# Three of twelve modulation quads summed on the Vector engine from a buffer of their own, with TensorE's chunks in two others; low weights of the last key-value pairs ahead of a rotation

## The reference

```python
silu_c = jax.nn.silu(c)
silu_cctx = jax.nn.silu(c_ctx)
for i in range(DEPTH_2):
    sh1, sc1, g1, sh2, sc2, g2 = jnp.split((silu_c @ mod_w[i] + mod_b[i])[:, None, :], 6, axis=-1)
    a_lat = modulate(rms_norm(h_lat, norm_mix_g[i]), sh1, sc1)
    csh1, csc1, cg1, csh2, csc2, cg2 = jnp.split(silu_cctx @ mod_w[i] + mod_b[i], 6, axis=-1)
...
kv = (rms_norm(kv_lat, kv_norm_g) @ w_kv_up).reshape(b, n, MLA_HEADS, MLA_NOPE + MLA_V)
k_nope = rms_norm(kv[..., :MLA_NOPE], kn_nope_g)
q = (rms_norm(q_lat, q_norm_g) @ w_q_up).reshape(b, n, MLA_HEADS, MLA_NOPE + MLA_ROPE)
```

## Time and profile before

| | |
|---|---|
| median of 3 runs | 1856.75 us (1855.55 to 1859.64) |
| the profiled execution | 1841.65 us, its span 1839.8 us |
| TensorE busy | 1697.2 us, 92% of the span |
| DVE busy | 1140.1 us, 62% |
| ACT, POOL busy | 584.4 and 584.1 us, 32% each |
| loads of the modulation weights by POOL | 48 of 1 MB, on queue 0 |
| bytes moved | 515.93 MB, 280 GB/s over the span |

### The profile page before, as it was taken

One profiled execution on the slowest core, in us unless ns is written; L12 is line 12 of the kernel. 1 busy time (PEld: TensorE's weight loads), 2 busy tenths in 40 slices (PEclk: granted clock), 3 DMA queues, 4 the chain that ended last, 5 costly groups with the idle time before them and its releaser, 6 DMA issues.

```text
span 1839.8 us, 24801 instructions
## 1 busy us (share of the span) xinstructions
PE 1697.2 (92%) x9782; PEld 1322.6 (72%) x9782; DVE 1140.1 (62%) x2086; ACT 584.4 (32%) x926; POOL 584.1 (32%) x570
## 2 busy tenths in 40 slices
PE   7999999998879898799869878999999999999999
PEld 6876688876536355566536656989999865579997
DVE  4344347877687787767777668575553436635553
ACT  4444333221121212111211113444332545634332
POOL 0111100776667676557767761000000010000000
PEclk9999999999999999899989999999999999999999
DMA  8999776999999999999999995845555322035553
GB/s 274 314 324 312 265 258 190 404 409 409 409 408 385 409 410 408 399 357 409 407 409 409 409 401 211 278 145 183 188 190 168 94 78 94 1 115 183 183 185 134
DMA packets 223420, 515.93 MB, mean 280 GB/s; under 512 B 13324, under 2 KB 122204, under 8 KB 223324
## 3 DMA queue, kind: packets, MB, share of 16 engines
q0 software_dynamic: 86784, 318.80, 44.7%
q1 hardware_dynamic: 136192, 195.71, 31.2%
q10 hardware_dynamic: 348, 0.11, 0.0%
HBM read 513.53 MB, written 1.05 MB: 280 GB/s over the span
## 4 chain that ended last, share of the span: by engine, by line
PE 57%; DMA 22%; DVE 9%; POOL 5%; issue 3%; ACT 2%; SPq 0%; DVEq 0%; ACTq 0%; POOLq 0%
DMA more<-in_peer_v_dram,idx 12%; PE bank L937 10%; PE bank L940 9%; PE bank L938 9%; DMA more<-in_peer_u_dram,idx 7%; POOL more L831 5%; PE wide L1351 4%; PE bank L1299 4%; DVE more L2542 2%; PE wide L1086 2%; DMA weights<-in_w_in_dram 2%; PE bank L891 2%; PE bank L1582 1%; PE wide L1628 1%; PE bank L1012 1%
## 5 line engine op out<-in xcount | busy, mean ns | idle before, releaser
L2151 DVE TENSOR_TENSOR low_weights<-weights,high_weights 128x2048 fp32r<-128x2048 f32 x107 | 245.1, 2292 | 307.5 <-ACT high_weights L1737 307.2
L2542 DVE CUSTOM_DVE_ANT_0 more<-more,wide 128x1024 f32<-128x1024 f32 x256 | 310.9, 1219 | 149.7 <-DMA more<-in_peer_u_dram,idx 147.6
L937 PE MATMUL bank<-high_input,high_weights 128*128 128x256 f32 x1264 | 360.4, 285 | 7.8 <-DVE low_input L2151 6.7
L938 PE MATMUL bank<-high_input,low_weights 128*128 128x256 f32 x1296 | 363.6, 281 | 0.0
L940 PE MATMUL bank<-low_input,high_weights 128*128 128x256 f32 x1264 | 357.0, 282 | 0.0
L831 POOL DMA_INDIRECT more<-in_peer_u_dram,idx x256 | 285.7, 1116 | 197.7 <-DVE dots L2542 88.3
L1351 PE MATMUL wide<-more,rstd 128*128 128x512 f32 x476 | 242.5, 645 | 75.6 <-ACT rstd L1925 58.9
L1737 ACT ACTIVATE high_weights<-weights 128x2048 fp32r<-128x2048 f32 x107 | 204.8, 1915 | 303.5 <-DMA weights<-in_ffn_w_down_dram 78.9
L831 POOL DMA_INDIRECT more<-in_peer_v_dram,idx x256 | 252.8, 987 | 115.2 <-issue 68.2
L937 PEld LDWEIGHTS bank<-high_input,high_weights 128*128 128x128 f32 x1264 | 239.1, 189 | 17.3 <-issue 17.1
L938 PEld LDWEIGHTS bank<-high_input,low_weights 128*128 128x128 f32 x1296 | 248.0, 191 | 0.5 <-issue 0.5
(11 more groups left out here) (308 smaller groups left out, 2399.4 us busy)
## 6 DMA issues: line engine op xcount, KB each, us to landing
weights<-in_ffn_w_down_dram SPq DMA_DIRECT2D x33, 1024.0 KB, 4.9
weights<-in_ffn_w_gate_dram SPq DMA_DIRECT2D x30, 1024.0 KB, 5.4
weights<-in_ffn_w_up_dram SPq DMA_DIRECT2D x30, 1024.0 KB, 5.4
weights<-in_conv_w_in_dram SPq DMA_DIRECT2D x24, 1024.0 KB, 9.2
weights<-in_w_in_dram SPq DMA_DIRECT2D x20, 1024.0 KB, 9.8
nrm<-in_mod_w_dram POOLq DMA_DIRECT2D x14, 1024.0 KB, 8.3
sq<-in_mod_w_dram POOLq DMA_DIRECT2D x13, 1024.0 KB, 7.3
h_ctx<-in_mod_w_dram POOLq DMA_DIRECT2D x13, 1024.0 KB, 7.8
```

Of the source, the lines that this page charges most:

```text
L937: first = nc.tensor.matmul(out, cut(high), hi, start=start, stop=False, **more_args)
L938: nc.tensor.matmul(out, cut(w_lo[b]), hi, start=False, stop=False, **more_args)
L2151: return nc.vector.tensor_tensor(out, a, b, op)
L2542: nc.vector.tensor_tensor_reduce(u, u, wide[0][:, :], 1.0, 0.0, ALU.mult, ALU.add, dots[:, n % 16:n % 16 + 1]).then_inc(s_dot, 1)
```

## The change

Twelve of the 48 chunks are taken from TensorE and given to DVE: those of the second place in steps 0 to 3, 6 to 9 and 12 to 15 (numbers 6, 8, 10, 12, 18, 20, 22, 24, 30, 32, 34, 36). They now carry quads 8, 9 and 10. DVE multiplies the rows of a chunk by the conditioning value of each partition and adds them up in `mod_sum`, two instructions of 128x1024 a chunk, in the step after the chunk's own, behind the low weights; TensorE then sums over partitions with eight matmuls against ones (`mod_turn_sum`) in steps 5, 11 and 17. DVE's chunks land in h_ctx alone, TensorE's in nrm and sq in turn, and the loads are in the order of `LOAD_ORDER`, in which a DVE chunk stands one tensor chunk later than its number says. The load of a DVE chunk waits for the sum of the DVE chunk before, that of a tensor chunk for the use of the tensor chunk two before (`mod_rank` numbers TensorE's chunks). In MLA half of the query scaling moves behind pair 0, and `low_kv(2)` moves from the start of the last quad to before the rotation of the third.

```diff
+VECTOR_BEATS = [0, 1, 2, 3, 6, 7, 8, 9, 12, 13, 14, 15]
+VECTOR_MODS = [FIRST + 2 * _s for _s in VECTOR_BEATS]
+TENSOR_MODS = [_j for _j in range(48) if _j not in VECTOR_MODS]
+TENSOR_QUADS = list(range(8)) + [11]
+VECTOR_QUADS = [8, 9, 10]
+VECTOR_TURNS = {5: 8, 11: 9, 17: 10}
+LAST_TURN = 7
+LOAD_ORDER = sorted(range(LATE_MODS[0]), key=lambda j: j + 1.5 * (j in VECTOR_MODS)) + LATE_MODS
...
+def mod_home(j):
+
+    return 2 if j in VECTOR_MODS else mod_rank(j) % 2
...
@@ pool @@
-            for j in range(BUBBLE_MODS[0]):
+            for j in LOAD_ORDER:
...
-                elif j >= 3:
-                    pool.wait_ge(s_mod_used, j - 2)
-                quad, part = j // MOD_PARTS, j % MOD_PARTS
+                elif j in VECTOR_MODS[1:]:
+                    pool.wait_ge(s_mod_added, VECTOR_MODS.index(j))
+                elif j not in VECTOR_MODS and mod_rank(j) >= 2:
+                    pool.wait_ge(s_mod_used, mod_rank(j) - 1)
+                quad, part = mod_part(j)
...
-                    nc.gpsimd.dma_start(mod_w[j % 3], src).then_inc(m_landed[j % 3], 16)
+                    nc.gpsimd.dma_start(mod_w[mod_home(j)], src).then_inc(m_landed[mod_home(j)], 16)
@@ tensor @@
+            def mod_turn_sum(quad):
+
+                pe.wait_ge(s_mod_added, MOD_PARTS * (VECTOR_QUADS.index(quad) + 1))
+                wait_free(pe, "mod_turn", quad)
+                b = bank_of("mod_turn", quad)
+                for m in range(8):
+                    mm = nc.tensor.matmul(bank[b][:, 2 * m:2 * m + 2], mod_sum[:, m * P:(m + 1) * P], ones[:, 0:2],
+                                          start=True, stop=True)
+                mm.then_inc(full[b], 1)
...
-                for j in beat_mods(s)[1:]:
+                for j in tensor_mods(s, False):
                     mods(j)
+                for quad in vector_turns(s):
+                    mod_turn_sum(quad)
@@ vector @@
+            def add_modulation(j):
+
+                quad, part = mod_part(j)
+                v.wait_ge(m_landed[mod_home(j)], 16 * (VECTOR_MODS.index(j) + 1))
+                if part == 0 and quad > VECTOR_QUADS[0]:
+                    wait_full(v, "mod_turn", quad - 1)
+                for k in range(2):
+                    rows, by = mod_w[mod_home(j)][:, k, :], cvec[:, 2 * part + k, 0:1]
+                    if part == k == 0:
+                        settle(nc.vector.tensor_scalar(mod_sum, rows, by, None, ALU.mult))
+                    else:
+                        settle(nc.vector.scalar_tensor_tensor(mod_sum, rows, by, mod_sum, ALU.mult, ALU.add))
+                v.sem_inc(s_mod_added, 1)
...
             for s in range(HALVES + 1):
...
                 if s in BEAT and BEAT[s] + 3 < 20:
                     low("qkv", BEAT[s] + 3)
+                for j in vector_mods(s - 1) if s >= 1 else []:
+                    add_modulation(j)
@@ vector, MLA @@
-            for k in range(6):
-                last = scaled(qlat[:, k, :], qlat[:, k, :], vcol("q_lat", k), root)
-            last.then_inc(s_qlat, 1)
...
+            scale_query(range(3))
...
             for n in range(KV_FIRST):
                 kv_pair(n)
+                if n == 0:
+                    scale_query(range(3, 6))
...
-                if i == QUADS - 1:
-                    low_kv(2)
...
                 v.sem_inc(s_roped, 1)
+                if i == QUADS - 2:
+                    low_kv(2)
                 if i == QUADS - 1:
                     kv_pair(KV_FIRST)
                 rotate(("rope_turn", i), here, turned[:, i % 2, :])
```

More of the change, by code:

```diff
@@ L72, in beat_mods, with tensor_mods, vector_mods, vector_turns @@
     return [j for j in (FIRST - 1 + 2 * s, FIRST + 2 * s) if j < LATE_MODS[0]]
+def tensor_mods(s, first):
+    return [j for j in (beat_mods(s)[:1] if first else beat_mods(s)[1:]) if j not in VECTOR_MODS]
+def vector_mods(s):
+    return [j for j in beat_mods(s) if j in VECTOR_MODS]
+def vector_turns(s):
+    return [VECTOR_TURNS[s]] if s in VECTOR_TURNS else []
+def mod_rank(j):
+    return TENSOR_MODS.index(j)
+def mod_home(j):
+    return 2 if j in VECTOR_MODS else mod_rank(j) % 2
+def mod_part(j):
+    if j in VECTOR_MODS:
+        n = VECTOR_MODS.index(j)
+        return VECTOR_QUADS[n // MOD_PARTS], n % MOD_PARTS
+    return TENSOR_QUADS[mod_rank(j) // MOD_PARTS], mod_rank(j) % MOD_PARTS
 def turned_after(j):
-    return [(j - 5) // MOD_PARTS] if j >= 5 and j % MOD_PARTS == 1 else []
+    if j in VECTOR_MODS:
+        return []
+    n = mod_rank(j)
+    return [(n - 5) // MOD_PARTS] if n >= 5 and n % MOD_PARTS == 1 else []
 def mod_turns(j):
@@ L94 @@
         EARLY += mod_turns(_j)
+    EARLY += [("mod_turn", _q) for _q in vector_turns(_s)]
     if _s >= 4 and _s % 2 == 0:
@@ L381, in program @@
         logit = view(more, 12288, 3, PACK)
-        prob = view(more, 14848, 3, PACK)
-        expo = view(more, 16384, 3, PACK)
-        soft = [rstd[:, c, 0:PACK] for c in range(2)] + [view(more, 17920, PACK)]
+        prob = view(more, 14592, 3, PACK)
+        expo = view(more, 15744, 3, PACK)
+        soft = [rstd[:, c, 0:PACK] for c in range(2)] + [view(more, 16896, PACK)]
+        mod_sum = view(more, 17280, D)
         prob_t = [std[:, c, 0:PACK] for c in range(2)]
@@ L1078, in mod_chunk @@
                 else:
-                    buffer = mod_w[j % 3]
-                    pe.wait_ge(m_landed[j % 3], 16 * (j // 3 + 1))
-                if part == 0 and quad:
-                    pe.wait_ge(s_mod_left, quad)
+                    buffer = mod_w[mod_home(j)]
+                    pe.wait_ge(m_landed[mod_home(j)], 16 * (mod_rank(j) // 2 + 1))
+                if part == 0 and rank:
+                    pe.wait_ge(s_mod_left, rank)
                 for k in range(2):
@@ L1832, in _ @@
                     leave_chunk(BEAT[s])
-                for j in beat_mods(s)[1:]:
+                for j in tensor_mods(s, False):
                     mod_rows(j)
+                for quad in vector_turns(s):
+                    leave_modulation(quad)
                 if s >= 4 and s % 2 == 0:
@@ L2665, in _, with scale_query @@
             tt(kpe[:, T:2 * T], kpe[:, T:2 * T], turned[:, 0, :], ALU.add).then_inc(s_kpe, 1)
[L2667 to L2670 removed]
+            def scale_query(ks):
+                by = inverse_root("q_ones", T)
+                for k in ks:
+                    last = scaled(qlat[:, k, :], qlat[:, k, :], vcol("q_lat", k), by)
+                if ks[-1] == 5:
+                    last.then_inc(s_qlat, 1)
+            scale_query(range(3))
             def kv_pair(n):
```

41 lines of the change are left out of this document (20 added, 21 removed).

## The result

The changed kernel takes **1899.08 us** (median of 4 runs, 1894.71 to 1903.64) against 1858.2 for the kernel before (4 runs, 1855.55 to 1865.57): ratio 1.0221, 95% interval 1.0197 to 1.0244. It is slower by 41 us; 1898 was forecast.

What follows compares the result with a forecast made beforehand. TensorE was taken to set the attention stage's time, with loads arriving just in time. Waits less removed work +35.1, clock +9.9, MLA -3.4 gave +41.6: 1883 us from the profiled 1841.65, plus 0.8% 1898, range 1867 to 1928.

Steps and rivals of the forecast that it cites:

- The chain: Attention: tensor chunk's load stands in POOL's queue behind one awaiting DVE's sum, landing 8.6 us after it; +35.1 net, chance 0.81.
- group 1: Attention steps 0 to 3: TensorE waits for the loads of chunks 11 and 14, 18.0 us in all.
- group 2: Attention steps 6 to 9: TensorE waits until chunk 26 lands at 182.4, wanted at 163.5, 18.9 us.
- group 3: Attention steps 12 to 15: TensorE waits until chunk 38 lands at 226.2, wanted at 213.0, 13.2 us.
- clock: Attention: TensorE runs at 1.2 GHz after long waits; four such spells of 3.3 us less one of before, +9.9 us.
- MLA: MLA stage: TensorE's waits of 2.29 us (low weights) and 1.28 us (scaled keys) go, taken as -3.4 us.
- before's 0.8%: Whole kernel: median 1856.75 us lies 0.8% above the profiled 1841.65, added to 1883 to give 1898.
- The lower bound: Whole kernel: loads land in 5.4 us, waits 32.6 (+17.6 net), no slow spell, full 3.6 in MLA: 1871, with scatter 1867.
- Rival (a): Attention: loads land fast since DMA idles while TensorE waits; +20.8, or 1878 us; chance 0.10.
- Rival (b): Attention: loads are never late if chunk 6's sum ends before 83.6; -12.5, or 1844 us; chance 0.06.
- Rival (c): Attention: the DMA link is the bound, saved time becomes waiting for bytes, only MLA counts; 1853 us; chance 0.03.
- The signs: Waits of 5 to 11 us at chunks 11, 14, 23, 25, 26, 37, 38; lower clock, DMA share below 0.85, MLA waits gone.

Runs made afterwards that it cites:

- e4: Changed kernel with TensorE multiplying by zeros ahead of chunks 11, 13, 14, 23, 25 and 37: no change in time, stage ended 0.6 us sooner.
- e1: Kernel before with only the MLA part of the change (query scaling in halves, moved low_kv(2)): ratio 0.9992 to before, its interval holds 1.
- e2: Changed kernel without its MLA part, so the modulation part alone: +45.9 us against its runs of before.
- e3: Changed kernel with each vector chunk's load two tensor chunks later in POOL's queue (offset 3.5) and each vector quad's turn one step later: 1881.35 us.
- e6: Changed kernel with DVE's sum put ahead of the low weights of its step instead of behind them: 1879.67 us.
- e7: Changed kernel with load offset 5.5, DVE's sums in steps 0-3, 5-8, 10-13, turns in 6, 11, 17: both forecasts missed, time not in the text.
- e11: Changed kernel with two quads on DVE, offset 3.5, vector chunks in steps 0, 1, 3, 5, 7, 9, 12, 14, turns in 8, 18: within 1865 to 1877 us.
- e12: e11 with products by zeros on TensorE ahead of chunks 5, 13 and 37 and behind the turn of step 8: 5.2 us faster than e11.

## Why the prediction was right

**The chain, its first link.** The load of chunk 11 was issued at 96.42 and its matmul began at 104.05, 7.6 us; the same for chunks 14, 23 and 25 is 7.7, 7.4 and 7.35, and 9.7 and 9.2 for chunks 13 and 37. I took 7.8 from the earlier trace rows, and 8.6 from the end of the sum: 95.34 to 104.05 is 8.7. The Trainium skill's rule ("DMA: Bandwidth & Descriptors", "Anatomy of one DMA — SWDGE (gpsimd) path"), by which such a load takes 4.4 us, an estimate from that page, would have been too short a price here: none of the six is under 7.3. They do not test the rule for a load alone. Each had another load of 1 MB issued 0.7 us ahead of it, and between issue and matmul the DMA share was 0.78 to 0.90 for the first four.

**The round of DVE's chunks.** I had sums in a row at best 10.5 us apart, with 7.9 from sum to landing. POOL issued DVE's loads 10.3, 8.5, 10.0 and 10.3 us apart in groups 2 and 3, close to that, but not for the reason given. DVE's loads landed in 5.8 us (median; 5.5 to 8.2 from 90 to 262 us), and only three of the 12 sums waited for theirs, 7.4 us in all. Most of the time DVE's other work of the step stood ahead of the sum. So the price of DVE's loads was too high and the step's own length made up for it, which is luck. A small slip of the sum stands beside it: chunks 18 and 30 are the first of their quads, and by the prediction's own prices their sums take 2.0 us, not 2.6.

**The waits.** Group by group:

```
                 forecast            measured
group 1          18.0                19.9  (9.75 at chunk 11, 2.01 at 13, 8.13 at 14)
group 2          18.9                14.2  (7.94 at 23, 6.28 at 25, none at 26)
group 3          13.2                 5.6  (at 37; none at 38)
clock            13.2 (3.3 before)   26.3  (3.2 before)
waits and clock  63.3                66.0
```

At chunk 11, 10.7 us were forecast and 9.75 came. The sum ended 1.0 us later than I had it, since its low weights begin at 91.07 and not earlier by the chunk that is gone: they hang on ACT's high half. TensorE wanted the chunk 2.1 us later than I had it, too, behind a wait of 1.34 us at chunk 5 and a spell that cost 1.7.

**The step that was mis-sized is the clock: four spells were counted, eight were there and a ninth began at the stage's end**, 23.1 us more than before in place of 9.9. The price of one was right, 3.3 us on the average; their number was not. Behind each of the five long waits TensorE ran at 1.2 GHz for 3 to 9 us of work; two waits of 1.3 and 2.0 us had a spell too, and one spell, from 220 to 234 us, had no wait ahead of it. Too little clock and too much waiting (39.8 where 50.1 stood) are one error twice: work at half clock fills the time until the next load lands, as chunks 26 and 38 show, which did not wait, and e4, where the filling gained nothing. The prediction says that the next wait takes the loss up; it should have taken the spell off that wait, not left it out of the count. The stage's end was forecast at +45.0 and measured at +46.4 (+42.2 from e1 to e2, the same two codes in that stage). Where the chain binds, the split does not matter to it. But the spell from 220 to 234 us, 6.8 us lost, lies between the second chain's waits and the third's and was in no term, and the third group's waits came 7.6 us short. That these two cancel is in part luck.

**MLA.** -3.0 in place of -3.4: the waits of 2.29 and 1.28 us went and one of 0.54 came.

**From the profiled execution to the median.** I added before's 0.8% (15 us) without knowing what it was. Nearly all of it was the stretch from 307 to 370 us, 14 us or more quicker in that profile than in the 13 others; that the addition came out right was luck: the 14 us might as well have lain in the stage that the change touches.

**The bounds and the rivals.** The lower bound's waits of 32.6 us do not follow from the steps as given: 2.4 us off each of eight loads leaves 30.9. Rival (a), loads that land fast, did not come for TensorE's chunks. Rival (b), never late, failed at its own point: the sum of chunk 6 ended at 95.34 and not before 83.6. Rival (c) neither: the DMA share fell to 0.70. The signs all came but two, the waits at chunks 26 and 38; the wait of 2.0 us at chunk 13 was not among them.

What the result rests on beyond the first link is shown by edits in two points: the order (e3, -18) and the low weights ahead of the sum (e6, -19). The third, one buffer for DVE, is read from e7's waits, which went to DVE, and was not tested by itself. That the removed work never shows, even in e11 and e12, is the clock's doing in part. In e11 the stage's work without the clock's loss is 7.9 us shorter than before's, the idle time 7.4 longer and the clock's loss 14.8 greater. With 8 chunks less TensorE has gaps of 1 to 4 us, and each such gap in e11 but one was followed by a spell of half clock or began in one. How much of it is that and how much the two buffers that are left for TensorE's chunks was not tried apart.

## What to carry to other kernels

Before work goes to an idle engine, write down its buffer's round (release, issue, landing, work) and compare it with the step; and look what else stands behind its load in the issuing queue, for a load that waits stops them all. A busy engine that loses work in small pieces gets gaps, and in these runs the longer of TensorE's gaps and some of the short ones were followed by a spell (in e11 five of the six of 1 us or more): price idle time and clock together, as one time to the next landing, not one after the other. And look at two profiles of the kernel before, where one lies far from the median of the runs.

## What was not expected of the hardware

In the stretch behind 330 us, where POOL's gathers have filled the DMA engines, TensorE stood between matmuls of one product with no releaser, in 13 profiles of 14. The changed kernel's timeline and stretch, and DMA queues from 383 to 392 us:

```profile
383.31 0.38 PE L937 MATMUL bank<-nrm,weights 128*128 128x256 f32 x1 [1.21 <-issue]
385.41 0.59 PE L937 MATMUL bank<-nrm,weights 128*128 128x256 f32 x1 [1.72 <-issue]
```

```profile
388.00:398.00 10.00, 6.16 (x15) 4.45 (x15) 3.10 (x6) 3.26 (x6) 3.51 (x4) 0.50 1.03 411
```

```profile
q0 software_dynamic: 1010, 3.68, 102.4%
```

ACT stood 21.75 us there, and SP 22.9, released by nothing that the profile names. POOL's gathers had the engines to themselves from 383 to 392 us, and no instruction packet is seen in them. Nor is a weight load, but none was under way: SP issued one at 369.83 and the next at 393.17, and when those had been issued the weights' queue got 91% from 396 to 400 us. In before's profile the stretch from 320 to 345 us, the corresponding one, had 31.5% for the weights' queue and three instruction packets, and no stall. Late instructions would fit three engines that stand at once; that they are the cause is not shown. The Trainium skill ("Runtime: NRT & Kernel Launch", "Instruction fetch mechanics") has each engine fetch its instructions by a DMA queue of its own, and calls the cost "mostly hidden"; if that is what stalled here, it cost 14 us or more in all but one profile.
